# Two gate products placed among the query, key and value groups, and the next product placed in the last recurrence round, of a three-block kernel on one core

## What is computed

```python
# first block, parallel_mixers (h: 512 x 1024)
proj = h @ w_in
qkv, z, a, bt, glu, gates = jnp.split(proj, offs, axis=-1)      # qkv: 3072 columns
qkv = jax.nn.silu(causal_depthwise_conv(qkv, gdn_conv_qkv))     # 4 taps
q, k, v = ...                                                   # q, k: l2-normalised per head
o = chunk_gated_delta_rule(q, k, v, g, beta)
y_a = (rms_norm(o, gdn_norm_g) * jax.nn.silu(z)) @ w_gdn_out
c = c_lin * jax.nn.sigmoid(c_gate)                              # from glu
c = causal_depthwise_conv(c, conv_dw_w) + conv_dw_b             # 31 taps
c = jax.nn.silu(layer_norm(c, conv_ln_g, conv_ln_b))
y_c = c @ w_conv_out + b_conv_out
g_a, g_c = jnp.split(gates, 2, axis=-1)
y = jax.nn.sigmoid(g_a) * y_a + jax.nn.sigmoid(g_c) * y_c
return y @ w_mix_out

# third block, odd_layer
p = h @ w_in
pc, zc, fd, zd = jnp.split(p, ODD_SPLITS, axis=-1)
yc = rwkv7_bidir_branch(pc, ...) * jax.nn.silu(zc)              # 16 heads, two directions
yd = fourier_branch(fd, fnet_w) * jax.nn.silu(zd)
return jnp.concatenate([yc, yd], axis=-1) @ w_out
```

## Time and profile before

| | us |
|---|---|
| median of 3 runs | 5427.48 |
| lowest, highest | 5421.26, 5431.49 |
| the profiled execution | 5430.62 |
| its span, first to last instruction | 5428.8 |
| PE busy in it | 5071.4 (93%) |
| DVE busy | 1668.5 (31%) |
| ACT busy | 866.2 (16%) |
| mean granted clock of PE | 0.963 |

### The profile page before, as it was taken

The page is one execution under the profiler, slowest core; times in us unless marked ns, Lnnn a source line. Parts: engine busy times, 40 slices in busy tenths (PEclk is TensorE's granted clock), DMA queues, the critical chain, the costliest instruction groups (busy, mean ns, idle before and its releaser), DMA issues.

```text
span 5428.8 us, 48478 instructions
## 1 busy us (share of the span) xinstructions
PE 5071.4 (93%) x21092; PEld 2906.6 (54%) x21092; DVE 1668.5 (31%) x2883; ACT 866.2 (16%) x1478; POOL 146.6 (3%) x228
## 2 busy tenths in 40 slices
PE   8999998989999999999999999899999788888998
PEld 3444444675464443465555444344444777777843
DVE  1211873340211001462442100221010555555511
ACT  0001012121021000311221100010001333333211
POOL 0000000000000000000000000000000111111000
PEclk9999998999999999899999999999999999999999
DMA  5433441003221222111111222222221000000021
GB/s 199 150 108 54 68 69 40 1 1 85 93 78 62 78 74 74 47 39 62 33 47 47 70 78 78 70 70 70 75 66 57 1 1 1 1 1 1 14 83 47
DMA packets 284883, 311.14 MB, mean 57 GB/s; under 512 B 7168, under 2 KB 277632, under 8 KB 281472
## 3 DMA queue, kind: packets, MB, share of 16 engines
q1 hardware_dynamic: 284672, 308.04, 19.1%
HBM read 305.92 MB, written 2.10 MB: 57 GB/s over the span
## 4 chain that ended last, share of the span: by engine, by line
PE 51%; DVE 4%; ACT 2%; issue 0%; DMA 0%; DVEq 0%; ACTq 0%; SPq 0%
PE ps L261 31%; PE ps L579 3%; PE ps L592 2%; PE ps L566 1%; PE ps L1726 1%; PE ps L2420 1%; PE ps L306 1%; PE ps L342 1%; PE ps L2438 1%; PE ps L599 1%; PE ps L2659 1%; PE ps L1445 1%; PE ps L2177 1%; PE ps L1434 1%; PE ps L2351 1%; PE ps L2340 0%
## 5 line engine op out<-in xcount | busy, mean ns | idle before, releaser
L261 PE MATMUL ps<-main,w 128*128 128x512 f32 (+1 forms) x8016 | 3473.4, 594 | 94.0 <-ACT main L782 23.5
L261 PEld LDWEIGHTS ps<-main,w 128*128 128x128 f32 x8016 | 1529.1, 192 | 1967.4 <-issue 1939.2
L579 PE MATMUL ps<-main,w 128*128 128x128 f32 x1536 | 224.1, 294 | 4.0 <-DVE main L2524 2.2
L579 PEld LDWEIGHTS ps<-main,w 128*128 128x128 f32 x1536 | 201.8, 205 | 16.7 <-issue 7.0
L535 DVE SCALAR_TENSOR_TENSOR main<-main,ps 128x512 f32<-128x512 f32 x44 | 30.3, 689 | 553.5 <-PE ps L261 553.5
L592 PE MATMUL ps<-main 128*128 128x128 f32 x1440 | 195.7, 293 | 2.4 <-DVE main L638 2.4
L488 DVE SCALAR_TENSOR_TENSOR main<-main,params_sb 128x512 f32<-128x512 f32 x256 | 192.5, 752 | 9.1
L592 PEld LDWEIGHTS ps<-main 128*128 128x128 f32 x1440 | 184.3, 206 | 10.6 <-issue 7.5
L612 ACT COPY main<-ps 128x512 f32<-128x512 f32 x180 | 105.5, 586 | 522.6 <-PE ps L566 522.6
L566 PE MATMUL ps<-consts_sb,main 128*128 128x128 f32 x944 | 141.9, 277 | 7.0 <-DVE main L622 6.8
L546 DVE SCALAR_TENSOR_TENSOR main<-main,ps 128x512 f32<-128x512 f32 x32 | 22.0, 688 | 399.9 <-PE ps L261 399.9
(11 more groups left out here) (415 smaller groups left out, 3866.7 us busy)
## 6 DMA issues: line engine op xcount, KB each, us to landing
w<-in_w_in SPq DMA_DIRECT2D x58, 1024.0 KB, 6.5
w<-in_e_w_in SPq DMA_DIRECT2D x28, 1024.0 KB, 5.0
main<-in_ada_w SPq DMA_DIRECT2D x24, 1024.0 KB, 9.2
w<-in_ffn_wg SPq DMA_DIRECT2D x22, 1024.0 KB, 5.2
w<-in_ffn_wu SPq DMA_DIRECT2D x22, 1024.0 KB, 5.3
w<-in_o_w_in SPq DMA_DIRECT2D x20, 1024.0 KB, 5.3
w<-in_ffn_wd SPq DMA_DIRECT2D x16, 1024.0 KB, 4.8
w<-in_w_up SPq DMA_DIRECT2D x16, 1024.0 KB, 5.4
```

The lines of the kernel that those rows point to most:

```text
L261: i = pe.mm(PS[b][:, 0:n], wv[:, k, f * 128:(f + 1) * 128], g.X(kg + k), start=kg + k == 0, stop=kg + k == g.nk - 1)
L579: t = pe.mm(one(PS[b], i), one(MT, i), one(Dm, i), start=True, stop=True)
```

## The change

Two places change.

In the mixers, `gc0` goes behind group `qkv4` and `gc1` behind `qkv6`, each ahead of that group's head sums. Their four output tiles now take banks of the ring 1 to 7. On ACT their Sigmoids move along: two behind q14 and two behind q20.

In the odd layer, the aside of round 15 makes one step per turn where it made two, and goes on with the first two pairs of `G_zc`, in slots 2 and 3 behind `G_f`. Their four Silus stand in ACT's aside. `pe_odd` starts with pair 4 of `G_zc`, and the Fourier steps behind it are interleaved in a slightly different order. "after rwkv" and "dft" now stand between the second and the third block of `G_zc` in SP's list.

```diff
@@ pe_mixers
         for f in range(8):
             run(pe_gemm(pe, G_qkv[f]))
+            if f in (4, 6):
+                run(pe_gemm(pe, G_gc[f // 2 - 2]))
             if f > 1:
...
         banks.only(range(8))
-        for i in range(2):
-            run(pe_gemm(pe, G_gc[i]))
@@ act_mixers, at the end of each group f
-        for f in range(4):
-            gates(a, f)
+            if f in (4, 6):
+                gates(a, f - 4)
+                gates(a, f - 3)
@@ pe_odd
-        run(pe_pair(pe, G_zc, 0))
         input_here("dft")
+        run(pe_pair(pe, G_zc, 4))
         dft_d(0)
-        run(pe_pair(pe, G_zc, 2))
+        run(pe_pair(pe, G_zc, 6))
         dft_s(0)
-        run(pe_pair(pe, G_zc, 4))
+        dft_d(1)
+        run(pe_pair(pe, G_zf, 0))
         fnet(0)
-        dft_d(1)
-        run(pe_pair(pe, G_zc, 6))
         dft_s(1)
-        run(pe_pair(pe, G_zf, 0))
-        fnet(1)
         dft_d(2)
         run(pe_pair(pe, G_zf, 2))
+        fnet(1)
         dft_s(2)
@@ rw_rounds
-            streams += [products(e, r + 2) if r < 14 else aside(e, r)] * 2
+            streams += [products(e, r + 2) if r < 14 else aside(e, r)] * (2 if r < 15 else 1)
@@ pe_rw_aside
+        for slot in (2, 3):
+            weights.only((slot,))
+            yield from pe_pair(pe, G_zc, 2 * slot - 4)
@@ act_rw_aside
+        def gate(f, b):
+            a.wait_ge(*at("mm", "zc", f))
+            a.act(t512[f], b, ACT.Silu).then_inc(a.inc(sem["act", "odd"], "out", "zc", f), 1)
+        for j in (0, 2):
+            yield from out_pair(G_zc, j, gate)
```

More of the change, by code:

```diff
@@ L773, in act_mixers, with gates @@
             a.act(G2(f % 2), bank("glu gate", f), ACT.Sigmoid).then_inc(a.inc(s, "out", "glu gate", f), 1)
+        def gates(a, f):
+            a.wait_ge(*at("mm", f"gc{f // 2}", f % 2))
+            a.act(GC(f), bank(f"gc{f // 2}", f % 2), ACT.Sigmoid).then_inc(a.inc(s, "out", f"gc{f // 2}", f % 2), 1)
         for f in range(8):
@@ L789, in act_mixers @@
                     a.act(t512[4 + q % 4], Q(q), ACT.Square).then_inc(a.inc(s, "qk square", q), 1)
-        def gates(a, f):
-            a.wait_ge(*at("mm", f"gc{f // 2}", f % 2))
-            a.act(GC(f), bank(f"gc{f // 2}", f % 2), ACT.Sigmoid).then_inc(a.inc(s, "out", f"gc{f // 2}", f % 2), 1)
-        for f in range(4):
-            gates(a, f)
+            if f in (4, 6):
+                gates(a, f - 4)
+                gates(a, f - 3)
         act_head_root(a, "qk", 64)
@@ L2247, in fnet @@
             a.copy(YF(g), bank("fnet", g)).then_inc(a.inc(s, "out", "fnet", g), 1)
-        zc(0, 1)
+        zc(4, 5)
         dft_d(0)
-        zc(2, 3)
+        zc(6, 7)
         dft_s(0)
-        zc(4, 5)
+        dft_d(1)
+        zf(0, 1)
         fnet(0)
-        dft_d(1)
-        zc(6, 7)
         dft_s(1)
-        zf(0, 1)
-        fnet(1)
         dft_d(2)
         zf(2, 3)
+        fnet(1)
         dft_s(2)
```

## The result

| | before | changed |
|---|---|---|
| median of the first comparison, us | 5431.49 (5421.26 to 5437.94, 5 runs) | 5399.09 (5398.97 to 5409.55, 5 runs) |
| ratio of it | | 0.9948 [0.9932, 0.9963] |
| the same two programs, measured again on one chip, us | 5423.71 (5415.8 to 5431.81, 29 runs) | 5412.24 (5399.01 to 5413.92, 7 runs) |
| ratio of that | | 0.9974 [0.9963, 0.9985] |
| profiled execution of the first comparison, us | 5430.62 | 5398.97 |

Measured again it is 5412.24. By the medians the gain is 32.4 us in the first comparison and 11.5 in the second, where 14.7 was forecast. Three questions follow: what the mixers gave, what the last round gave, and what is left. Three groups of rows answer them.

What follows compares the result with a forecast made beforehand. PE was taken as the bound, busy 5071.4 of 5428.8 us, so moved work counts only in its holes. Mixers 7.7 plus last round 7.0 gave 14.7; median 5427.5 - 14.7 = 5412.8 us, range 5404 to 5424.

Steps and rivals of the forecast that it cites:

- What comes behind moves as a whole: Code behind the mixers' spreading: shifts as a whole, with no gain or loss of its own counted.
- the best case of 12.1: Mixers: gain of 12.1 us if the group behind gc0 loses its extra 1.8 and the mean starts at full clock.
- the shift proper: Mixers: gc0 ahead of the head sums makes them 13.8 us later, passed on in full to DVE.
- mean and small product: Mixers, ahead of the spreading: mean 7.0 us, restart at lower clock 2.6, small product 11.0.
- the two Sigmoids and their load: Mixers, between Silu of q20 and copy of q21: table load and two Sigmoids put 2.5 us on the path.
- Rival (c): Mixers: head sums have slack, DVE doesn't shift, the whole hole closes; 29.3 us instead of 7.7, 5391; chance 0.06.
- Rival (d): Mixers: clock stays at 1.2 GHz through mean, small product, spreading and gc2; loses 14 us, 5434; chance 0.06.
- The length of the round: Round 15, through the spreading: 60.1 us together, ending 13.6 later with three more tiles made.
- The time from SP's first issue to the landing: Last round: pair 4's weight block lands 12.2 us after SP's start, bounds 5.3 and 15.1.
- DVE's last two instructions and SP follow 1.64 later: 5215.4: End of recurrence: SP starts the loads 1.64 us after the spreading ends at 5213.8, behind DVE's last two instructions.
- Rival (b): Last round: pair 4's weights land late, gain 4 us or less, ACT's wait longer; 5416 to 5419; chance 0.13.
- Rival (a): Mixers: DVE's shift eats all the gain, clock drops in groups and mean; 7.6 us less, 5420; chance 0.13.

Runs made afterwards that it cites:

- the mixers alone: Kernel before with only gc0 behind group 4 and gc1 behind group 6, with their Sigmoids, odd layer as before: 5413.65 us, ratio 0.9978.

## Why the prediction was right and wrong

**Neither the first measurement nor the terms came out.** The forecast was 14.7 us of gain. The first comparison gave 32.4, and its two traces 31.6, which is 16.9 more: 7.2 more in the mixers (14.9 against 7.7), 6.8 less in the last round (0.2 against 7.0), and 16.5 in code between them. For that code the prediction has one sentence, "What comes behind moves as a whole", a term put at nothing without a reason, and it is what moved the total out of the range. The repeat gave 11.5 by the medians and 14.1 by the ratio (0.26% of 5423.7). That this is near 14.7 is luck: 7.7 were to come from the mixers and 7.0 from the last round, and the runs show about 12 and 0.

**Mixers, the mechanism right, two terms mis-sized.** Over the six traces with these edits as they stand the spreading starts at 875.1 on average (872.99 to 877.77), over the three without at 886.8: 11.7, near the best case of 12.1. The trace of the changed kernel shows where the terms were off, with two rows of before beside it, the head sums ahead of group 4 and the group:

```profile
707.55 3.11 PE L455 MATMUL ps<-consts_sb,tmp 128*128 128x1 f32 x24
710.52 23.85 PE L261 MATMUL ps<-main,w 128*128 128x512 f32 x48
```

The head sums of group 5 came at 768.89; before, 759.19. Of these 9.7 the stage's earlier start makes -0.65; the shift proper is 10.35, not 13.8. The pair took its 13.7 (34.58 against 20.85 for a group at the full level), but the group that it was joined to had taken 23.85 before, 3.0 more than its matmuls need, and that dip of the clock wasn't there now, nor the one of 0.4 in the head sums ahead of it. My prediction quoted group 5 (22.54, the same in both) and never looked at group 4, whose row stands in none of its groups. The repeats show that such dips wander: the sums of group 5 came at 755.6 to 759.9 in the three traces without the mixers' edits and at 768.3 to 773.1 in the six with them. By the averages the shift is 12.2, so about half of what this term missed in the first traces was the luck of two executions. Second, mean and small product: from start to start 17.6, against the 20.6 counted. Before, they took 17.7 with no hole ahead. I took the 11.03 of the small product for its cost at the full clock, though it contained a dip, and added a restart of 2.6 on top; now the small product took 9.19 and the mean 8.72, so the restart had replaced the dip. With the 0.65 these two make the 7.1 by which the spreading came ahead of 880.7. The rest is as the steps said: the shift passed through ACT and `conv31(6)` (it starts at 774.36, not 778), the two Sigmoids and their load put 2.4 on DVE's path (an idle time of 3.57 where 1.17 is usual; 2.5 counted), the switch cost its load alone (845.02 to 846.30, the activation starts at 846.32; the 1.38 us of drain that the Trainium skill states in "ScalarE: Activation LUTs", What ACT_TABLE_LOAD costs, didn't show here either, since the load starts 0.02 behind the end of a Silu), and one hole of some 24 (25.8) stood ahead of the mean. Rival (c), no shift of DVE, is refuted for the change: the square of q13 waited 9.7 longer and `conv31(6)` started 9.7 later. The kernel with the gates one group later is what it would have been, and 8.0 us of the hole stay even there. Rival (d), the clock at its lower level through all that follows, didn't come: 17.6.

**Last round, the mechanism failed in one step.** The length of the round was right: 60.4 from 5122.28 to 5182.66, predicted 60.1, with the hole of 2.5 and its price. The time from SP's first issue to the landing was right: 12.4, predicted 12.2, and so was the restart. The step that failed is its beginning, "DVE's last two instructions and SP follow 1.64 later: 5215.4". I had taken from before that DVE's last instruction ends the recurrence for SP. The change itself altered that: Silus and a pair in the aside are part of `rw_rounds`, so the fence "rwkv" of ACT and PE moved behind them, 6.2 us later than DVE's end. In place of a hole of 6.9 stood one of 13.2, and of the 7.0 expected 0.2 was left. The kernel with the fence on DVE alone shows the cause: the hole is 8.5 there. The prediction asked of every moved piece which queue it is moved past, and not which fence it is moved into. The landing time had been named as the place to look; counted from DVE's end it came 18.6 later, outside the 5 to 15 given.

Rival (b), the weights late, is what happened, by a mechanism that it did not name, with part 2 at 0 where it said "4 or less". Rival (a), part 1 eaten, is refuted.

**The range.** It took its width from the terms alone. Two medians of the changed kernel lay 13 us apart, by the clock in code that neither part touches, and the first comparison fell on the short side for the changed kernel and on the long side for before. A range for a single comparison would have needed that, downward and upward.

## What to carry to other kernels

When work is moved into a stage, read which fences close that stage, for every engine: a fence on "all engines done" takes in the new work and holds back transfers that need none of it. Moved work shortens nothing while a transfer decides the end of the hole; bring the transfer forward first, then the work pays. To judge an edit in a kernel whose clock varies between executions, measure its own stretch between two marks in the program, and not the whole time, where 13 us come and go. In the last round such a stretch repeated within 0.3 us; it isn't free of the clock either (1.4 us in one kernel), and the spreading of the mixers starts anywhere within 4.8 us in six traces with one order. So read PE's idle and busy time of the stretch apart: a wait shows in the idle time, the clock in the busy time.

## What the runs showed of the hardware

The first-product-to-end stretch of before, of the changed kernel and of the ones that don't alter its critical path repeats within 0.3 us (274.9 to 275.2 in seven traces), while the stretch from 2577 takes 307.9 us at a granted clock of 0.97 and 315.4 or 316.7 at 0.94, with the same idle time of PE. The runs of the changed kernel and of the mixers alone don't spread evenly; most lie in one of two groups 13 us apart.

The issue of one and the same 2 MB transfer (`dft_s`) took SP 0.44 us in the changed kernel and 1.28, 1.38, 1.55 and 1.70 in the four kernels that issue it second, right at DVE's end. Where a weight block goes first (before, and "dft" behind pair 4's block), `dft_s` takes 0.43 and the issue of the 256 KB behind it (`fnet`) is the long one, 1.40 to 1.65 against 0.58 elsewhere. Nothing was tried on its cause.

What PE loses after a hole did not grow with the hole: mean and small product together took 17.6 after 25.8 us, 17.6 after 12.0, 20.8 after 8.0 and 17.6 after 6.9.
